# Trunk kernel (two hybrid layers, 512 tokens): first MLP pass in eight plain tiles, products combined within PSUM

## What is computed

```
h = h + mixer(rmsnorm(h))                    # even: attention + mLSTM; odd: SSD + RWKV-7
n = rmsnorm(h)                               # 512 x 1024
h = h + square(relu(n @ w_up)) @ w_down      # w_up 1024 x 4096, w_down 4096 x 1024
```

## Time and profile before

| | |
|---|---|
| median of three runs | 1362.69 us |
| profiled execution, its own time | 1364.89 us |
| its span, first to last instruction | 1363.1 us |
| PE busy | 1274.8 us, 94% |
| DVE / ACT / POOL busy | 811.5 / 633.2 / 620.5 us |
| HBM traffic | 79 GB/s over the span |

### The profile page before, as it was taken

One profiled execution on the slowest core, in us unless ns is written; L12 is line 12 of the kernel. 1 busy time (PEld: TensorE's weight loads), 2 busy tenths in 40 slices (PEclk: granted clock), 3 DMA queues, 4 the chain that ended last, 5 costly groups with the idle time before them and its releaser, 6 DMA issues.

```text
span 1363.1 us, 20055 instructions
## 1 busy us (share of the span) xinstructions
PE 1274.8 (94%) x7837; PEld 1085.3 (80%) x7837; DVE 811.5 (60%) x1137; ACT 633.2 (46%) x1024; POOL 620.5 (46%) x681
## 2 busy tenths in 40 slices
PE   6999988879999999999999999999968999999997
PEld 5777666778888988978788778888768897888976
DVE  4537665893472743744689956476785273572753
ACT  5345665553261542634582535643535263361541
POOL 4653324827346174364455533222746517265081
PEclk9999988889999999999898989899979999999999
DMA  9322101334153251422212311001414234153311
GB/s 275 93 78 62 53 12 46 108 93 125 30 152 96 67 147 35 124 61 64 78 49 76 81 59 47 2 2 32 124 53 135 61 108 125 40 143 81 94 31 62
DMA packets 165293, 109.22 MB, mean 80 GB/s; under 512 B 4570, under 2 KB 162512, under 8 KB 165200
## 3 DMA queue, kind: packets, MB, share of 16 engines
q1 hardware_dynamic: 164784, 107.88, 28.3%
q0 software_dynamic: 416, 0.07, 0.0%
HBM read 105.83 MB, written 2.10 MB: 79 GB/s over the span
## 4 chain that ended last, share of the span: by engine, by line
PE 65%; DVE 22%; issue 6%; ACT 6%; DMA 1%; SPq 0%; DVEq 0%; ACTq 0%
PE ps L1200 8%; PE ps L1201 8%; PE ps L1202 8%; PE ps L1080 5%; PE ps L1081 5%; PE ps L1082 5%; PE ps L1180 3%; PE ps L1182 3%; PE ps L1181 3%; DVE hid_lo L2378 3%; PE ps L1067 3%; DVE arena L2372 2%; DVE wx_lo L2339 2%; DVE relu L2372 1%; DVE w_lo L2339 1%
## 5 line engine op out<-in xcount | busy, mean ns | idle before, releaser
L953 POOL TENSOR_TENSOR w_lo<-raw_w,w_hi 128x256 fp32r<-128x256 f32 x248 | 214.4, 895 | 277.1 <-ACT w_hi L1685 277.1
L2383 DVE TENSOR_TENSOR h<-h,ps 128x512 f32<-128x512 f32 x64 | 44.0, 687 | 219.9 <-PE ps L1202 219.9
L1080 PE MATMUL ps<-hn_hi,w_hi 128*128 128x512 f32 x368 | 154.3, 419 | 0.1
L1081 PE MATMUL ps<-hn_lo,w_hi 128*128 128x512 f32 x368 | 147.2, 400 | 0.0
L1082 PE MATMUL ps<-hn_hi,w_lo 128*128 128x512 f32 x368 | 147.0, 399 | 0.0
L1022 POOL TENSOR_TENSOR w_lo<-y_mix,w_hi 128x256 fp32r<-128x256 f32 x80 | 67.2, 870 | 148.7 <-ACT w_hi L1751 148.7
L1022 POOL TENSOR_TENSOR wx_lo<-y_mix,wx_hi 128x256 fp32r<-128x256 f32 x80 | 69.0, 893 | 137.3 <-ACT wx_hi L1751 137.3
L1751 ACT ACTIVATE wx_hi<-raw_w 128x1024 fp32r<-128x1024 f32 x56 | 59.2, 1057 | 109.5 <-PE ps L1202 82.9
L1200 PE MATMUL ps<-hid_hi,w_hi 128*128 128x512 f32 x256 | 101.5, 397 | 6.6 <-DVE hid_lo L2378 6.6
L1200 PE MATMUL ps<-hid_hi,wx_hi 128*128 128x512 f32 x256 | 100.7, 393 | 7.1 <-DVE hid_lo L2378 7.1
L1751 ACT ACTIVATE w_hi<-raw_w 128x1024 fp32r<-128x1024 f32 x56 | 59.2, 1057 | 99.0 <-PE ps L1202 83.0
(11 more groups left out here) (463 smaller groups left out, 3598.6 us busy)
## 6 DMA issues: line engine op xcount, KB each, us to landing
raw_w<-in_w_up SPq DMA_DIRECT2D x32, 512.0 KB, 4.4
y_mix<-in_w_up SPq DMA_DIRECT2D x32, 512.0 KB, 4.4
raw_w<-in_w_down SPq DMA_DIRECT2D x32, 512.0 KB, 3.6
y_mix<-in_w_down SPq DMA_DIRECT2D x32, 512.0 KB, 4.4
raw_w<-in_o_w_in SPq DMA_DIRECT2D x27, 512.0 KB, 3.8
raw_w<-in_e_w_in SPq DMA_DIRECT2D x19, 512.0 KB, 3.8
raw_w<-in_e_w_out SPq DMA_DIRECT2D x8, 512.0 KB, 3.6
raw_w<-in_o_w_out SPq DMA_DIRECT2D x8, 512.0 KB, 3.5
```

The costliest lines, as they stand in the source:

```text
L953: nc.gpsimd.tensor_tensor(w_lo[:, n % CUT, ks], raw_w[:, n % RING, ks], w_hi[:, n % CUT, ks].bitcast(F32), ALU.subtract).then_inc(w_cut, 1)
L1080: mm(o, a_hi, b_hi, start=(k == 0), stop=False)
L1081: mm(o, a_hi, b_lo, start=False, stop=False)
L2383: V.tensor_tensor(h[:, j, :], h[:, j, :], ps[:, D_BANK + j % 2, :], ALU.add).then_inc(added, 1)
```

## The change

Of the four passes of each layer, the first (i = 0) makes its up half without the seven-product scheme: eight **plain** tiles (`plain_up`) of 24 matmuls, 512 columns wide, three for each of eight input tiles, into PSUM banks 0 to 5 by turns. Their hidden tiles go through `hidden_whole` (relu and norm straight from PSUM, square, high, low). The cuts of all 16 weight tiles of that pass are POOL's; no weight sums are made for it. Passes 1 to 3 keep the scheme, so the differences are still wanted, but first in pass 1: they are made behind the first hidden tiles (`gain_pair`, `part`, `part_high_of`, `part_low_of`, `third_low`) and no longer in `project_out`, whose low parts are now all full tiles.

In every pass the first two down tiles are split in two (`down_part`): tile 0 and tile 1 over the first four hidden tiles, then both over the other four.

In passes 1 to 3, `quarter_of` writes the combination back into its PSUM bank, and the relu reads it there. On ACT, the copy of m5 for p = 1 stands ahead of the hidden quarter c21 of p = 0. At the end of layer 0 two cuts of the next layer's weights stand one and two steps earlier (`cut_next`).

The diff, cut to its core:

```diff
+def cut_on_pool(i, u):
+    return i == 0 or u >= NUP - 2
+
...
+                whole_up = dram["w_up"][layer].rearrange("(k p) c -> p k c", p=P)
+                for u in range(2 * KT):
+                    if u < RING:
+                        sp.wait_ge(w_cut, PARTS * (n0 - RING + u + 1))
+                    else:
+                        unit_cut(sp, layer, 0, u - RING)
+                    load_tile(PLAIN_AT[u % 4], whole_up[:, :, u * SW:(u + 1) * SW] if u < KT else down_tile(0, u - KT))
+                unit_cut(sp, layer, 0, 2 * KT - 4)
+                load_up("A0", 1)
...
+                for u in range(2 * KT):
+                    low_unit(0, u)
+                for i in range(1, 4):
...
-                    if i == 0 and q == "m2" and p == 0:
-                        drained(pe, "out", layer, KT - 1)
...
+                    if i > 1 and u == 0:
+
+                        pe.wait_ge(relued, 32 * layer + 8 * i)
...
+                        if i == 1 and k == 0 and q in ("m5", "m7"):
+                            pe.wait_ge(part_low, 5 * layer + (4 if q == "m5" else 5))
...
+                def plain_up(j):
+                    hi_, lo_ = (v.rearrange("p (k c) -> p k c", c=SW) for v in cut_buffers(layer, 0, j))
+                    o = ps[:, j % D_BANK, :]
+                    if j >= D_BANK:
+                        pe.wait_ge(relued, 32 * layer + j - D_BANK + 1)
+                    for k in range(KT):
+                        unit_cut(pe, layer, 0, j, k // 2 + 1)
+                        if j == 0:
+                            pe.wait_ge(normed, KT * (3 * layer + 2) + k + 1)
+                        mm(o, hi_[:, k, :], hn_hi[:, k, :], start=(k == 0), stop=False)
+                        mm(o, hi_[:, k, :], hn_lo[:, k, :], start=False, stop=False)
+                        ins = mm(o, lo_[:, k, :], hn_hi[:, k, :], start=False, stop=(k == KT - 1))
+                    ins.then_inc(u_done, 1)
+
...
+                def down_part(i, j, ks):
+                    hi_, lo_ = (v.rearrange("p (k c) -> p k c", c=SW) for v in cut_buffers(layer, i, ups(i) + j))
...
+                    if ks[0] == 0:
+                        n = 32 * layer + KT * i
+                        if j >= 2:
+                            pe.wait_ge(added, n + j - 1)
+                        elif n:
+                            pe.wait_ge(added, n)
+                    for k in ks:
+                        unit_cut(pe, layer, i, ups(i) + j, k // 2 + 1)
...
+                    if ks[-1] != 3:
+                        ins.then_inc(u_done, 1)
...
+                    for u in range(ups(i)):
+                        if i:
+                            up_unit(i, u)
+                        else:
+                            plain_up(u)
+                            if u == 0:
+                                norm(2 * layer + 1)
+                    if i:
+                        first_k, other_k = DOWN_K[:4], DOWN_K[4:]
+                    else:
+                        first_k, other_k = [0, 1, 2, 3], [4, 5, 6, 7]
+                    for ks in (first_k, other_k):
+                        for j in range(2):
+                            down_part(i, j, ks)
+                    for j in range(2, KT):
+                        down_part(i, j, list(range(KT)))
...
+                    drained(act, "out", layer, k)
+                    high_gained("mlp_norm", 8 * layer + k)
+                    if k == KT - 1:
...
                         high_unit(layer, 0, 2)
-                    drained(act, "out", layer, k)
...
-                    A(spare[:, k % 2, :], h[:, k, :], ACT.Copy, scale=gain).then_inc(gained, 1)
...
+                def gain_pair(pair):
+
+                    if pair:
+                        act.wait_ge(parted, 4 * layer + pair)
+                    for k in (2 * pair, 2 * pair + 1):
+                        A(spare[:, k % 2, :], h[:, k, :], ACT.Copy, scale=col_a("mlp_norm", 8 * layer + k)
+                          ).then_inc(gained, 1)
+
+                def part_high_of(pair):
+
+                    act.wait_ge(parted, 4 * layer + pair + 1)
+                    A(d_hi[:, :, pair, :], d_parts[:, 1:4, :], ACT.Copy).then_inc(part_high, 1)
 
...
+                for u in range(KT):
+                    if u == 0:
+                        full(act, "out", layer, KT - 1)
+                        act.wait_ge(w_cut, PARTS * n0)
+                    high_unit(layer, 0, u + 3)
+                    if u == 0:
+                        norm(2 * layer + 1)
+                    hidden_whole(u)
+                    if 2 <= u <= 5:
+                        part_high_of(u - 2)
+                    if 1 <= u <= 4:
+                        gain_pair(u - 1)
+                for u in range(KT + 3, 2 * KT):
+                    high_unit(layer, 0, u)
+                    if u == KT + 3:
+                        act.wait_ge(parted, 4 * layer + 4)
+                        unit_done(act, layer, 0, KT - 1)
+                        A(hn_hi[:, 0:KT:2, HT:T], place(layer, "E1").rearrange("p (k t) -> p k t", t=HT), ACT.Copy
+                          ).then_inc(part_high, 1)
+                for u in range(4):
+                    high_unit(layer, 1, u)
...
                     high_unit(layer, i, 12)
+                    copy(i, "m5", 1)
                     hidden(i, "c21", 0)
-                    copy(i, "m5", 1)
                     high_unit(layer, i, 13)
...
+                    low_gained(3 * layer + 2, "mlp_norm", 8 * layer + k)
+                    sum_squares(2 * layer + 1, k)
...
+                def hidden_whole(j):
+                    t = relu_t[:, j % 2, :]
+                    unit_done(dve, layer, 0, j)
+                    if j >= 2:
+                        dve.wait_ge(hid_ready, hid_turn(layer, 0, j - 2))
+                    V.scalar_tensor_tensor(out=t, in0=ps[:, j % D_BANK, :], scalar=0.0, in1=rms_t, op0=ALU.max,
+                                           op1=ALU.mult).then_inc(relued, 1)
+                    dve.wait_ge(hid_high, hid_turn(layer, 0, j))
+                    V.tensor_tensor(hid_lo[:, j, :], t, hid_hi[:, j, :].bitcast(F32), ALU.subtract
+                                    ).then_inc(hid_ready, 1)
...
+                    if pair:
+                        dve.wait_ge(part_low, 5 * layer + pair)
+                    third = place(layer, "E1").rearrange("p (k t) -> p k t", t=HT)
+                    V.tensor_tensor(third[:, pair, :], flat[:, 0:HT], flat[:, HT:T], ALU.subtract)
+                    link(V.tensor_tensor(d_parts[:, 1, :], flat[:, HT:T], flat[:, T + HT:], ALU.subtract))
+                    link(V.tensor_tensor(d_parts[:, 2, :], d_parts[:, 1, :], flat[:, 0:HT], ALU.subtract))
+                    V.tensor_tensor(d_parts[:, 3, :], flat[:, T:T + HT], d_parts[:, 2, :], ALU.add).then_inc(parted, 1)
...
+                    dve.wait_ge(part_high, 5 * layer + 5)
+                    V.tensor_tensor(hn_lo[:, 0:KT:2, HT:T], place(layer, "E1").rearrange("p (k t) -> p k t", t=HT),
+                                    hn_hi[:, 0:KT:2, HT:T].bitcast(F32), ALU.subtract).then_inc(part_low, 1)
...
+                        o = z
+                        ins = V.tensor_tensor(z, z, flat, ALU.subtract)
...
+                        o = x
+                        ins = V.tensor_tensor(x, flat, x, ALU.subtract)
...
+                        o = v
+                        ins = V.tensor_tensor(v, v, flat, ALU.add)
...
+                    V.scalar_tensor_tensor(out=t, in0=o.rearrange("p (a t) -> p a t", t=HT), scalar=0.0,
+                                           in1=over(rms_half, 1, 2), op0=ALU.max, op1=ALU.mult).then_inc(relued, 1)
...
+                norm(2 * layer + 1)
+                for j in range(KT):
+                    hidden_whole(j)
+                    if 2 <= j <= 5:
+                        part_low_of(j - 2)
+                    if 1 <= j <= 4:
+                        part(j - 1)
+                third_low()
+                for j in range(KT):
+                    add(0, j)
+                    if j >= 4:
+                        low_unit(1, j - 4)
```

277 lines of the change are left out of this document (108 added, 169 removed).

## The result

The changed kernel takes 1301.46 us (median of 4 runs, 1299.80 to 1302.21). The kernel before, four runs of it by now, takes 1363.16 (1361.07 to 1366.28), so the ratio is 0.954, interval 0.952 to 0.957: 61.7 us less. The forecast was 1311.6 with a range from 1305: the direction was right, the gain 10 us larger than the sum, and outside the range by 3.5 us.

A forecast was written before the change was run, and what follows sets the result against it. PE bounds the kernel, busy 1274.8 of 1363.1 us. Terms 34.2 - 2 + 13.7 + 5.2 = 51.1 us, taken from the profiled 1364.9, give 1313.8; less 2.2 for the runs' median, 1311.6, range 1305 to 1326.

The forecast's parts named there:

- the charge for DVE: Plain half and first down half: hidden tile 7 and first add just in time, so 1 us a layer charged, -2.
- the 0 for what lies outside the MLP: Output projection and mixers: the sum held no gain there; the moved differences were counted only at the MLP's head.
- Plain half, 34.2: First up half of each layer: plain tiles take 45.5 us against 62.6, nothing waits; 17.1 saved per layer, 34.2.
- The 41.4 us: Plain half: eight tiles at the skill page's 215.7 ns a matmul; two layers together 6 us less than forecast.
- Rival D: Plain tiles miss the down tiles' rate, or the clock falls after the norm: 3 to 4 us a layer, 1319; chance 0.12.
- a round of both is thus 6 to 8.9 us, I take 7.4, half way: Plain half: DVE's time for one hidden tile plus difference work; hidden tile 7 stands at 307, wanted at 307.3.
- Rival A: Plain half: DVE falls behind beside POOL's cuts; PE waits for hidden tile 7, 8.5 us a layer, 1327; chance 0.15.
- Split, 13.7: Heads of all eight down halves: more matmuls cover the wait for `hid_lo`; six at 1.77 us, two at 1.56.
- copy, 5.2: Six later up halves: copy of m5 ahead of c21 removes a PE wait of 0.87 us each, 5.2.
- Rival B: Down halves: the split hides nothing, because what was late moves too; 13.7 comes back, 1325; chance 0.06.
- PSUM combination, 0: Passes 1 to 3: between -0.6 and +0.7 us an instruction, all under the down split's cover, so 0.
- End of layer 0, 0: Two earlier cuts of the next layer's weights: PE has no wait listed there, so 0.

The follow-up runs named there:

- `before`: The kernel before, run again unaltered for a second trace: 1361.25 us, ratio 0.9996; over four runs by now 1363.16 us.
- `whole_down`: The changed kernel with the first two down tiles whole again, not split: 1306.99 us, ratio 0.961.
- `split_only`: The kernel before with only down tiles 0 and 1 split, copy of m5 as before: 1345.64 us, ratio 0.987.
- `sbuf_combine`: The changed kernel with the quarters combined into SBUF again, relu from two SBUF inputs: 1301.74 us, ratio 0.955.
- both ballast kernels: The changed kernel with two or four extra DVE adds, results unused, behind each of hidden tiles 1 to 4 of the plain half: 1315.39 and 1329.82 us.
- the POOL wait: The changed kernel with POOL waiting, in each later pass, for hidden quarter c12's low part before down tile 1's cut: 1301.3 us, ratio 0.955.
- the padding: The changed kernel with 64 bytes a partition left free ahead of `w_hi` and `w_lo`: 1314.9 us, ratio 0.962.

## Why the forecast missed

By the halves of the two MLPs and the medians, 61.7 us came together so: plain halves 34.7, first down halves 3.6, later down halves 12.1, later up halves 6.5, end of the output projection 1.3 (23.05 to 22.40 us, and the same in layer 1), and 3.5 of the mixers, which is what is left (the pair of traces has 6.7 there, and layer 1's mixer alone moves by more than 3.5 from run to run).

The mechanism held for each term of the sum; what failed are their sizes: first the charge for DVE, then the listed waits as prices, and the 0 for what lies outside the MLP.

- **Plain half, 34.2: right** (17.36 and 17.37 measured). The down tiles' rate carried over: 192 matmuls in 44.37 us, as I took, and 0.86 for the norm instead of 1.1. The 41.4 us that came from the figure in the Trainium skill (TensorE: Matmul & The Clock Gate, "Wait — 56ns, not 53.3ns?") did not; the row decided rightly. Rival D falls.
- **The charge of 2 for DVE: wrong.** The step that failed is "a round of both is thus 6 to 8.9 us, I take 7.4, half way". Measured 6.03, the low end, for the reason shown above; the margin was 4.7 us, not 0.3. Rival A falls. Its price was sound (8.5 us a layer for rounds of 8.9; 7.0 measured at 8.6), its place was not: the first thing to be late is down tile 1's cut.
- **Split, 13.7: 15.7 measured** (12.1 + 3.6), and **copy, 5.2: 6.5 measured.** Both terms took the listed wait as the price. A later down half gained 1.94 to 2.10 for 1.8 listed, an up half 0.95 to 1.34 for 0.87 listed. The steps of PE's starts over a wait show about a quarter of a us more than the list in each case read: 2.03 for 1.78 listed (`before`, 408.19), 1.12 for 0.86 (`before`, 394.91), 0.43 for 0.19 (`whole_down`, 386.61). Rival B falls. How much of the 15.7 is the split's hangs on the order: by itself it takes all of it (`split_only`), taken away last it costs 5.5 (`whole_down`). In the first pass the gain was the plain half's as much as the split's.
- **PSUM combination, 0: right in time beside the split, wrong in what it does.** By the low parts shown at `whole_down`, it would take most of the wait at the down heads away by itself; the split hides that. The relus fell from 1.22 to 1.31 beside POOL to 0.69, as forecast, and the time stayed. I did not see what follows when DVE's relus no longer slow POOL's row: the low part that still has two SBUF inputs may be kept out.
- **End of layer 0, 0: right.**
- **Outside the MLP, 0: wrong.** With the differences gone from `project_out`, its end became 0.65 us shorter a layer (before, PE waited 0.37 us there for a cut of POOL's); I had counted the move only at the MLP's head. In the mixers, unchanged but for that, the record shows less time at 1.2 GHz (layer 1's mixer of before, then of the changed kernel):

```profile
623.99:980.73 356.74, 348.31 (x2447) 288.15 (x2445) 253.93 (x396) 184.29 (x329) 148.15 (x162) 0.96 0.20 55
```
```profile
592.95:944.03 351.08, 340.52 (x2446) 281.25 (x2445) 247.81 (x386) 179.60 (x320) 147.89 (x161) 0.99 0.19 52
```

I cannot call this an effect of the change. Layer 1's mixer took 351 to 356.7 us over all traces. Of the 15 with the plain pass, eight stood near 351.2, four at 352.5 to 352.9, and `sbuf_combine` at 356.03 and both ballast kernels at 356.1; the four without it had 353.50 to 356.74. Why it varies stays open.

The gain above the sum of 51.1, 10.6 us, is then: charge 2, later down halves 1.5, up halves 1.3, first down halves and plain halves 0.5 each, output projection 1.3, mixers 3.5. Every one has the same sign. Without the 3.5 of the mixers, whose cause is open, the time would stand at the edge of the range, at 1305. My range went 6.6 us down from the forecast and 14 up; the low end allowed only the charge and 2 us of luck, and nothing for terms that I had priced too low.

No kernel beat the changed one by more than its runs differ. With the POOL wait it takes the same time (1301.3) and no low part is kept out in its trace, also with the padding (1301.4); that is the version to keep.

## What to carry over

Price the removal of a wait at the listed idle and, here, a quarter of a us more, and look in the work ahead of the stage for what the moved instructions cost there. Where two engines slow each other, read from the lists which of their instructions really meet before spreading one's busy share over the other. After making one engine independent of another, look for long unbroken rows on either, and where they slow each other, give an instruction that must get in between a wait on the other side.
